# Sorting turned blocks into partition groups through a scratch buffer in HBM, in a decoder trunk of two layers

## The reference

```
for i in range(2):
    h = h + mixer_i(rmsnorm(h, g_mix[i]))                 # ends in "@ w_out"
    xn = rmsnorm(h, g_ffn[i])
    h = h + (silu(xn @ w_gate) * (xn @ w_up)) @ w_down    # hidden width 5632
    g = sigmoid(rmsnorm(h, g_ple[i]) @ w_ple_gate[i])
    h = h + g * (p[i] @ w_ple_proj[i])                    # p[i]: 256 x 256
return rmsnorm(h, g_final)
```

## Time and profile before

| | |
|---|---|
| median of 3 runs | 2415.82 us (2414.81 to 2416.91) |
| the profiled execution's own time | 2416.15 us |
| its span, first to last instruction | 2414.4 us |
| granted TensorE clock, mean | 0.997 of full |
| TensorE, VectorE, ScalarE busy | 99%, 55%, 47% |
| read from HBM, written | 440.49 MB, 2.10 MB |

### The profile page before, as it was taken

One profiled execution on the slowest core, in us unless ns is written; L12 is line 12 of the kernel. 1 busy time (PEld: TensorE's weight loads), 2 busy tenths in 40 slices (PEclk: granted clock), 3 DMA queues, 4 the chain that ended last, 5 costly groups with the idle time before them and its releaser, 6 DMA issues.

```text
span 2414.4 us, 29406 instructions
## 1 busy us (share of the span) xinstructions
PE 2387.1 (99%) x10908; PEld 1974.2 (82%) x10908; DVE 1333.5 (55%) x1655; ACT 1128.5 (47%) x1467; POOL 3.2 (0%) x17
## 2 busy tenths in 40 slices
PE   8999999999999999999999999999999999999997
PEld 7888778888888888888888888888888888888886
DVE  5545666555554555444466677554555555544455
ACT  5425545544444444444454575454444434444454
POOL 0000000000000000000000000000000000000000
PEclk9999999999999999999999999999999999999999
DMA  7744445666766666655557455566766667655563
GB/s 219 235 119 120 123 137 174 182 202 183 226 203 197 216 189 210 202 191 191 191 186 237 146 163 169 191 187 194 218 196 205 212 183 230 201 191 192 191 207 134
DMA packets 250938, 455.42 MB, mean 189 GB/s; under 512 B 21816, under 2 KB 38240, under 8 KB 250720
## 3 DMA queue, kind: packets, MB, share of 16 engines
q1 hardware_dynamic: 250800, 454.18, 60.2%
q10 hardware_dynamic: 48, 0.02, 0.0%
HBM read 440.49 MB, written 2.10 MB: 183 GB/s over the span
## 4 chain that ended last, share of the span: by engine, by line
PE 96%; DVE 1%; ACT 1%; DMA 1%; SPq 0%; issue 0%; ACTq 0%; DVEq 0%
PE ps L1338 30%; PE ps L1340 30%; PE ps L1339 30%; PE ps L1292 1%; PE ps L1549 1%; PE ps L1462 1%; DMA raw<-in_w_in_rec_dram 1%; PE ps L1393 1%; ACT w_hi L571 0%; PE ps L1474 0%; DVE w_lo L816 0%; SPq L494 0%; PE ps L1499 0%; ACT junk L627 0%; PE ps L1500 0%
## 5 line engine op out<-in xcount | busy, mean ns | idle before, releaser
L816 DVE TENSOR_TENSOR w_lo<-raw,w_hi 128x1024 fp32r<-128x1024 f32 x820 | 996.0, 1220 | 996.5 <-ACT w_hi L571 992.4
L571 ACT ACTIVATE w_hi<-raw 128x1024 fp32r<-128x1024 f32 x820 | 859.5, 1054 | 1092.0 <-PE ps L1340 925.1
L1338 PE MATMUL ps<-w_hi,xa_hi 128*128 128x512 f32 x1664 | 647.9, 389 | 0.0
L1340 PE MATMUL ps<-w_hi,xa_lo 128*128 128x512 f32 x1664 | 647.4, 389 | 0.0
L1339 PE MATMUL ps<-w_lo,xa_hi 128*128 128x512 f32 x1664 | 647.3, 389 | 0.0
L1340 PEld LDWEIGHTS ps<-w_hi,xa_lo 128*128 128x128 f32 x1664 | 312.3, 188 | 65.1
L1339 PEld LDWEIGHTS ps<-w_lo,xa_hi 128*128 128x128 f32 x1664 | 312.3, 188 | 64.7
L1338 PEld LDWEIGHTS ps<-w_hi,xa_hi 128*128 128x128 f32 x1664 | 312.3, 188 | 64.4
L1338 PE MATMUL ps<-w_hi,xb_hi 128*128 128x512 f32 x864 | 349.0, 404 | 3.9 <-DVE xb_lo L879 2.3
L1340 PE MATMUL ps<-w_hi,xb_lo 128*128 128x512 f32 x864 | 338.1, 391 | 0.0
L1339 PE MATMUL ps<-w_lo,xb_hi 128*128 128x512 f32 x864 | 337.3, 390 | 0.0
(11 more groups left out here) (201 smaller groups left out, 1022.0 us busy)
## 6 DMA issues: line engine op xcount, KB each, us to landing
raw<-in_w_ffn_gate_dram SPq DMA_DIRECT2D x176, 512.0 KB, 4.5
raw<-in_w_ffn_up_dram SPq DMA_DIRECT2D x176, 512.0 KB, 4.5
raw<-in_w_ffn_down_dram SPq DMA_DIRECT2D x176, 512.0 KB, 4.1
raw<-in_w_in_attn_dram SPq DMA_DIRECT2D x88, 512.0 KB, 3.6
raw<-in_w_ple_gate_dram SPq DMA_DIRECT2D x64, 512.0 KB, 4.3
raw<-in_w_in_rec_dram SPq DMA_DIRECT2D x64, 512.0 KB, 4.1
raw<-in_w_out_attn_dram SPq DMA_DIRECT2D x32, 512.0 KB, 4.3
raw<-in_w_out_rec_dram SPq DMA_DIRECT2D x32, 512.0 KB, 4.0
```

The lines of the kernel that those rows point to most:

```text
L571: nc.scalar.activation(w_hi[:, s, 0:n], raw[:, s, 0:n], ACT.Copy).then_inc(hi_ready, 1)
L816: nc.vector.tensor_tensor(w_lo[:, s, 0:n], raw[:, s, 0:n], w_hi[:, s, 0:n].bitcast(F32), ALU.subtract).then_inc(lo_ready, 1)
L1338: nc.tensor.matmul(o, xh[:, k, tok], w_hi[:, s, wk], start=(k == 0), stop=False)
L1340: ins = nc.tensor.matmul(o, xl[:, k, tok], w_hi[:, s, wk], start=False, stop=(k == nkt - 1))
```

## The change

Every chunk whose result has to be transposed, apart from those of the mixers' phases, now takes one way. It is `move=True` for the up chunks, for all resid chunks and for ple0; `banks` and `split` fall away for resid and ple, and with them their transposes on TensorE. VectorE transposes in blocks of 32 x 32, out of stage for up chunks and out of h for the others, directly after the evacuation at slot 3. SP stores the blocks by 4 DMAs of 128 KB (32 partitions, 4 rows of 1 KB in each) into a scratch tensor in HBM, before the load of the slot with number 8 from the start of that next chunk, waits for them, and fetches them by 2 DMAs of 256 KB (128 partitions, 4 rows of 512 B in each) into stage, before load 9. ScalarE rounds and VectorE subtracts at slot 6, with the gain as a scale for h, as one instruction each for the FFN. Squares, root and mean square stay at slot 7.

```
-    resid = Kind("resid", "v", 2, True)
+    resid = Kind("resid", "v", move=True)
...
-        ple = Kind("ple", "v", 0 if last else 2, True)
+        ple = Kind("ple", "v", move=not last)
...
+        scratch = nc.dram_tensor("scratch", [4, 32, 4, NT * P], F32, kind="Internal").ap()
+        st_blocks = stage[:].rearrange("p m (a x) -> p m a x", a=4)
+        moved_all = st_blocks.rearrange("p m a (k t) -> p (m a) k t", k=4)
...
-            def move_hid(q, i):
-
-                sp.wait_ge(hid_turned, hid_no(q, i))
+            def store_blocks(q, i, r):
+
+                if not q.kinds[r].move:
+                    return
+                sp.wait_ge(blocks_turned, move_no(q, i, r))
                 for a in range(4):
-                    for c in range(4):
-                        sp.dma_start(st_blocks[32 * c:32 * c + 32, a], sg_blocks[32 * a:32 * a + 32, c]
-                                     ).then_inc(hid_moved, 16)
+                    sp.dma_start(scratch[:, :, a].rearrange("c d x -> d c x"), sg_blocks[32 * a:32 * a + 32]
+                                 ).then_inc(blocks_out, 16)
+
+            def fetch_tiles(q, i, r):
+
+                if not q.kinds[r].move:
+                    return
+                sp.wait_ge(blocks_out, move_no(q, i, r) * 64)
+                for m in range(NT):
+                    sp.dma_start(st_blocks[:, m], scratch.rearrange("c d a (m x) -> (c d) m a x", m=NT)[:, m]
+                                 ).then_inc(blocks_moved, 16)
...
+                    if j == 8:
+                        store_blocks(*prev)
+                    if j == 9:
+                        fetch_tiles(*prev)
+                    if j == 0 and (two := behind(q, i, r, 8)):
+                        store_blocks(*two)
+                    if j < 2 and (two := behind(q, i, r, 9 - j)):
+                        fetch_tiles(*two)
                     load_slot(q, i, r, j)
...
+            def round_tiles(q, i, r):
...
+                act.wait_ge(blocks_moved, move_no(q, i, r) * 32)
+                if q.gain is None:
+                    ins = nc.scalar.activation(by_blocks(hi, c), moved_all, ACT.Copy)
+                else:
+                    for k in range(4):
+                        ins = nc.scalar.activation(tile_by_blocks(hi, 4 * c + k), moved_tile(k), ACT.Copy,
+                                                   scale=gain_ap(q.gain, 4 * c + k))
+                ins.then_inc(tiles_hi, 1)
...
-                    if (c := hid_chunk(q, i, r, j, 1)) is not None:
-                        round_hid(*c)
+                    if j == 6:
+                        round_tiles(*prev)
...
+            def turn_blocks(q, i, r):
...
+                dve.wait_ge(evac["v"], evac_no(q, i, r)[1])
+                c = column(q, i, r)
                 for m in range(NT):
+                    rows = stage[:, m] if k.name == "up" else h[:, m, c * CW:(c + 1) * CW]
+                    dst = sg_blocks.rearrange("p c (m k t) -> p m c k t", k=4, m=NT)[:, m]
+                    ins = nc.vector.transpose(dst, rows.rearrange("p (k c d) -> p c k d", k=4, c=4))
+                ins.then_inc(blocks_turned, 1)
...
                     if j == 3:
                         evacuate(*prev)
-                    if prev[0].kinds[prev[2]].name == "up" and j == 4:
-                        turn_hid(prev[0], prev[1])
-                    if (c := hid_chunk(q, i, r, j, 2)) is not None:
-                        split_hid(*c)
+                        turn_blocks(*prev)
+                    if j == 6:
+                        split_tiles(*prev)
...
-                    elif q.src == "H":
-                        pe.wait_ge(hid_ready, hid_no(q.before, (2 * j + 1) // 4))
+                    elif q.before and q.before.per_move:
+                        pe.wait_ge(tiles_ready, move_no(*maker(q.before, (2 * j + 1) // 4)))
...
-                elif k.name in ("resid", "ple"):
-                    c = 2 * i + r
-                    transpose4(lambda m, f: h[:, m, c * CW + f * P:c * CW + (f + 1) * P], t0)
```

More of the change, by code:

```diff
@@ L64, with __init__ @@
 class Kind:
-    def __init__(self, name, evac, banks=0, split=False):
+    def __init__(self, name, evac, banks=0, split=False, move=False):
         self.name, self.evac, self.banks, self.split = name, evac, banks, split
+        self.move = move
 class Phase:
@@ L111, in build_phases @@
                         gain=2 + layer, dst="A", stat=1 + 3 * layer))
-        ph.append(Phase(f"ffn{layer}", 11, (8, 8), (Kind("gate", "a"), Kind("up", "v")), "A",
+        ph.append(Phase(f"ffn{layer}", 11, (8, 8), (Kind("gate", "a"), Kind("up", "v", move=True)), "A",
                         (0, 0), (f"w_gate{layer}", f"w_up{layer}"), first_turn=True, loop=True,
@@ L123, in build_phases @@
                         stat=6 if last else 3))
-    slot, va, turn, hi = 0, {"v": 0, "a": 0}, 8, 8
+    slot, va, turn, hi, move = 0, {"v": 0, "a": 0}, 8, 8, 0
     for p in ph:
@@ L133, in build_phases @@
         p.per_hi = sum(k.banks for k in p.kinds if k.split)
+        p.move0, p.per_move = move, sum(k.move for k in p.kinds)
+        move += p.per_move * p.pairs
         p.per_v = {e: sum(k.evac == e for k in p.kinds) for e in "va"}
@@ L168, in hi_no, with move_no, maker @@
     return i * p.per_hi + (p.hi0 + sum(k.banks for k in p.kinds[:r] if k.split))
+def move_no(p, i, r):
+    return i * p.per_move + (p.move0 + sum(k.move for k in p.kinds[:r + 1]))
+def maker(p, c):
+    return (p, c, 1) if p.loop else (p, *divmod(c, 2))
 def two_before(p, i, r):
@@ L342, in trunk @@
         turned, turn_hi, turn_used = sem("turned"), sem("turn_hi"), sem("turn_used")
-        hid_turned, hid_rounded, hid_ready = sem("hid_turned"), sem("hid_rounded"), sem("hid_ready")
-        hid_moved = sem("hid_moved")
+        blocks_turned, blocks_out, blocks_moved = sem("blocks_turned"), sem("blocks_out"), sem("blocks_moved")
+        tiles_hi, tiles_ready = sem("tiles_hi"), sem("tiles_ready")
         consts, ident_ready, gmix_in = sem("consts"), sem("ident_ready"), sem("gmix_in")
@@ L421, in trunk, with moved_tile, by_blocks, tile_by_blocks @@
         sg_blocks = sg[:].rearrange("p m c -> p (m c)").rearrange("p (c x) -> p c x", c=4)
[L422 to L440, removed]
+        scratch = nc.dram_tensor("scratch", [4, 32, 4, NT * P], F32, kind="Internal").ap()
+        st_blocks = stage[:].rearrange("p m (a x) -> p m a x", a=4)
+        moved_all = st_blocks.rearrange("p m a (k t) -> p (m a) k t", k=4)
+        def moved_tile(k):
+            return moved_all[:, :, k]
+        def by_blocks(t, c):
+            tiles = slice(4 * c, 4 * c + 4) if isinstance(c, int) else bass.ds(4 * c, 4)
+            return t[:, tiles, :].rearrange("p k (b t) -> p b k t", t=32)
+        def tile_by_blocks(t, kt):
+            return t[:, kt].rearrange("p (b t) -> p b t", t=32)
+        def column(q, i, r):
+            return i if q.loop else 2 * i + r
         block = ctx.enter_context(nc.Block())
@@ L457, in load_slot, with behind @@
                 sp.dma_start(dst, src).then_inc(raw_in[s], 16)
-            def move_hid(q, i):
-                sp.wait_ge(hid_turned, hid_no(q, i))
-                for a in range(4):
-                    for c in range(4):
-                        sp.dma_start(st_blocks[32 * c:32 * c + 32, a], sg_blocks[32 * a:32 * a + 32, c]
-                                     ).then_inc(hid_moved, 16)
+            def behind(q, i, r, n):
+                two = two_before(q, i, r)
+                one = (q, i, 0) if r else two_before(q, i, 1)
+                return two if two and one[0].slots[one[2]] == n else None
+            def store_blocks(q, i, r):
+                if not q.kinds[r].move:
+                    return
+                sp.wait_ge(blocks_turned, move_no(q, i, r))
+                for a in range(4):
+                    sp.dma_start(scratch[:, :, a].rearrange("c d x -> d c x"), sg_blocks[32 * a:32 * a + 32]
[7 more added lines that the diff above has]
+                                 ).then_inc(blocks_moved, 16)
             def load_vectors():
@@ L488, in run_chunk @@
                                      ).then_inc(x_in[j], 16)
-                    if (c := hid_chunk(q, i, r, j, 1)) is not None:
-                        move_hid(*c)
+                    if j == 8:
[6 more added lines that the diff above has]
+                        fetch_tiles(*two)
                     load_slot(q, i, r, j)
@@ L585, in evacuate @@
                         if m == 0 and not (isinstance(i, int) and i == 0):
-                            act.wait_ge(hid_moved, hid_no(q, i - 1) * 256)
-                        elif m == 0 and q.name == "ffn1":
-                            act.wait_ge(hid_moved, hid_no(q, -1) * 256)
+                            act.wait_ge(blocks_moved, move_no(q, i - 1, 1) * 32)
+                        elif m == 0:
+                            act.wait_ge(blocks_moved, q.move0 * 32)
```

(44 more changed lines are left out.)

## The result

| | before | after |
|---|---|---|
| median | 2415.93 us (4 runs, 2414.81 to 2416.91) | 2432.6 us (4 runs, 2428.16 to 2436.60) |
| profiled execution, its span | 2416.15, 2414.4 us | 2428.16, 2426.2 us |

The ratio is 1.0069, 95% interval 1.0050 to 1.0087: the change made the kernel 0.7% slower, where 0.5% faster was forecast. The runs scatter over 8 us, those of before over 2.

The account below looks back on a forecast made before the run. TensorE, busy 99% of the span, was taken as the bound. Removing transposes saves 18.2 us and waits return 6.4, a net 11.8 off 2416.15; predicted 2404.0 us against the median, range 2397 to 2422.

Parts of the forecast that it names:

- Removal, 18.2 us: TensorE transposes removed from 20 chunks of out0, down0, ple0, out1 and down1, 0.91 us each: 18.2 us saved.
- FFN chunks cost nothing: In 22 FFN chunks w_lo of slot 7 is ready at T + 17.0 against 19.04: slack 2.0 us, no cost.
- rival 4: SP's relief speeds FFN weight loads, freeing more than the transposes; chance under 0.02. The forecast gave that relief no value.
- Blocks ready at T + 5 and landed at T + 13.5: Moved chunks: transposed blocks ready, then back through HBM, at these us after T, the end of a chunk's last matmul.
- the sum: Added-up times of a moved chunk's chain of evacuation, transposes, stores and loads: tiles landed at T + 13.5, bounds 11.2 to 18.9.
- forecast at 0.4: Last chunk of out0, down0, out1, down1: tiles at T + 16.7 against 16.32, 0.4 us each, 1.6 in all.
- Slack 1.1, nothing: Twelve residual chunks inside a phase: w_lo of slot 7 at T + 17.9 against 19.04, so no cost.
- "4.8" for ple0: ple0's later evacuations: 2.1 and twice 0.4 us at slot 7, 1.9 at the boundary to xb, sum 4.8 us.
- nothing more: At the four residual phase ends, squares and root delay w_lo of slot 8 to T + 22.1, without further cost.
- the pair: ScalarE's rounding and VectorE's subtraction of the tiles at slot 6, with w_lo of slot 7 standing behind.
- 6.4 forecast: TensorE time returned by waits: 1.6 us at four residual phase ends plus 4.8 at ple0.
- Rival 2: Slower: ScalarE waits for loads at slot 6, the ring of four runs dry; decides from d = 1.3; chance 0.20.

Follow-up runs that it names:

- e6: Changed kernel with evacuation and block transposes ahead of slot 3's splits, stores and fetches one load earlier, rounding and subtraction behind slot 7: 2398.93 us, ratio 0.9926.
- e1: Changed kernel with only FFN chunks on the new path, residual and ple0 chunks transposed by TensorE as before: 2414.88 us, ratio 0.9997.
- e4: Changed kernel with rounding and subtraction of the tiles behind slot 7 instead of slot 6: 2412.34 us, ratio 0.9987.
- e7: Changed kernel with weight load 8 issued behind the two fetches instead of between stores and fetches: 2416.94 us, ratio 1.0004.
- e3: Changed kernel without SP's wait between stores and loads, the loads fetching other data from input x: 2432.18 us, ratio 1.0074.

## Why the prediction was wrong

- **Removal, 18.2 us: right.** e6, with nearly no waits, is 17.3 us below the before of its own runs (2416.22); its intervals between matmuls have 1.2 us more of waiting than before's.
- **FFN chunks cost nothing: right**, shown by e1 and by the idle-free window. ScalarE's wait for ffn_up weights fell from 118.9 to 8.8 us and was worth nothing, as said (rival 4).
- **Blocks ready at T + 5 and landed at T + 13.5: right for FFN chunks**, 8.8 instead of 8.5 us. Its make-up was half right: the queue behind load 8 was in the sum. But the residual chunks at boundaries had 10.3 (down0), 9.6 (down1) and 9.3 us (out1), up to 1.8 over the sum, and the sum took one value for all. That alone is most of the wait at ple0 and ple1, forecast at 0.4, measured 2.5 and 1.8. The rounding and subtraction took 3.4 us instead of the 3.2 of the rows before.
- **"Slack 1.1, nothing", "4.8" for ple0 and "nothing more": the step that failed.** Each chunk was reckoned from a T at which weights and engines stood ready, as in the trace of before. In the changed kernel w_lo of slot 7 waits for the tiles, the load of slot 11 for w_lo, and ScalarE's slot 3 (in ple0 slots 2 and 3) of the next chunk for that load and the ones behind it; evacuation stands behind them. In chunks of 8 and 9 slots a chain that ends late thus makes the next start 0.5 to 1.8 us late, even where it ended early enough for TensorE's slot 7, as in out1. In down, with 22 slots, the ring recovers and inner chunks lose nothing. The prediction had named what stood behind the pair, but followed it only as far as TensorE's own slot 7, not to the load that it releases. e4, which takes the tiles from in front of slot 7 and with them from in front of that load, gives back 20 us. ple0 with its boundary returned 10.4 us of waits instead of 4.8.
- **The parts of the miss.** TensorE's waits grew by 23.3 us, against 6.4 forecast. Taking from each wait the lateness of its chain's start puts 7.9 us down to late starts. Longer transfers and pairs than in the sum make 6.1, the first chunk of out0 2.3 and xb 0.6. This split is an estimate from one profile; no run isolates the late starts.
- **In out0 the squares stand ahead of w_hi of slot 7**, by the list's own order for attention phases; the sum had them behind. Its first chunk also shares the queue with the load of p_tok: its last store took 5.3 us to land, and TensorE waited 2.3 us.
- **The clock was left out**: 4.7 us of the 30.5.
- **Rival 2** has the sign, the place and the ring that runs dry. Its turning point, 1.3 us over the sum, was too far out: the transfers were 0.3 us over it in the median of the FFN chunks and 0.5 in the others. With what is dragged along, the even point lies about 0.5 us under the sum: e7, where ready blocks to rounding took 8.0 to 8.1 us, is level with before. The 2 us of an HBM access under high load (Trainium skill, "DMA: Bandwidth & Descriptors", "Latency and other measured facts") are neither shown nor ruled out here: e3 gained nothing by skipping the wait for the stores, but its loads read HBM too. That a wait can be surprisingly long with HBM as target (same page of the Trainium skill, "Anatomy of one DMA") doesn't show in the median: the 128 KB stores landed in 2.4 us, where 2.3 follow from that section's formula (an estimate, as the section gives it for DMAs that GpSimd issues, and these are SP's).

What stays open: why half clock follows some waits and not others (2.3 us at 406, yes; 2.5 at 1194, no; and the same wait of 2.3 us at 357 in both kernels, before yes, after no). The other runs of the changed kernel are 3.3 to 8.4 us slower than the profiled one. Their mean clock was 0.994, 0.995 and 0.994 against its 0.996, by which 2.4 to 4.9 us of it would be the clock (a rough estimate: that share of 2430 us); they have no profile that would show the rest.

## What to carry to other kernels

Where a new wait is put into an engine's hand-written order, follow what stands behind it until a buffer is released and the load that needs this buffer, and on to the chunk after; a slack computed for one chunk holds only if that ring has recovered by the next. A long latency is cheap if its chain starts early and its end is consumed behind the work that refills the ring: with the same transfers, starting the evacuation one weight block sooner made 1.007 into 0.994, and consuming one slot later besides 0.993. Before blaming a round trip, take its wait away once: here that gained nothing, and moving one load from in front of the fetches gained 0.4 us of landing.

## What the hardware showed beside

- From 380 us on the changed kernel has nine waits of 1.8 us or more on TensorE. At three of them (2.2 to 3.3 us long) the clock was granted at half for 3.4 us, beginning 1.5 and 1.3 us behind the wait's end and 0.1 us before it. Each costs some 1.5 us beside the wait itself (window 408 to 412: 0.60).
- Loads issued 1.6 us earlier (e3) landed no earlier (5.6 instead of 3.7 us from issue), with the DMA engines busy 0.96 of the time.
- Through HBM, 4 stores and 2 loads took 8.8 us for 512 KB; 16 transfers inside SBUF took 9.6 us to issue alone.
